# Prompt attention of a hybrid decoder step: operands and heads in one block, probability turn and values one head behind the scores, rope queries and values as fp32r triples

## The reference, cut to what matters

```
q = rms_norm(q_a) @ w_q_b            # 8 heads, 128 nope + 64 rope channels
q_rope = rope(q[..., 128:]) * SCALE ; krope = rope(krope)
q_lat = (q[..., :128] @ w_k_b) * SCALE        # 256 latent channels a head
s = q_lat @ ckv.T + q_rope @ krope.T ; s = where(causal, s, -inf)
p = softmax(s)
mla_out = (p @ ckv) @ w_v_b                   # 128 channels a head
mix = concat(mla_out, pool_out, cross_out) * silu(gate)
x = x + mix @ w_out
```

## Time and profile before

| | |
|---|---|
| median of 3 runs | 1042.87 us (1041.45 to 1044.06) |
| profiled execution, its own time | 1044.82 us |
| its span in the trace | 1043.0 us |
| mean granted PE clock | 0.971 |
| PE, matmul | 957.4 us busy, 92% of the span |
| PEld, weight load (overlaps PE) | 853.2 us, 82% |
| DVE | 543.4 us, 52% |
| ACT | 429.9 us, 41% |
| POOL | 99.1 us, 10% |
| DMA | 155.99 MB, mean 150 GB/s |

### The profile page before, as it was taken

One profiled execution on the slowest core, in us unless ns is written; L12 is line 12 of the kernel. 1 busy time (PEld: TensorE's weight loads), 2 busy tenths in 40 slices (PEclk: granted clock), 3 DMA queues, 4 the chain that ended last, 5 costly groups with the idle time before them and its releaser, 6 DMA issues. The chain is left out here.

```text
span 1043.0 us, 15821 instructions
## 1 busy us (share of the span) xinstructions
PE 957.4 (92%) x5821; PEld 853.2 (82%) x5821; DVE 543.4 (52%) x989; ACT 429.9 (41%) x700; POOL 99.1 (10%) x104
## 2 busy tenths in 40 slices
PE   5989999999899999999999897999558699999996
PEld 5967999999789999999999645888457588888884
DVE  3466244322366688878875264665556542233434
ACT  4774211132314576766664132544355442132310
POOL 0010014022000000000000010211454000000000
PEclk9999999999999999999999898999879799999998
DMA  9864432142714778788763341100243463314222
GB/s 364 287 220 141 154 119 74 62 130 85 294 64 129 245 246 250 241 244 248 240 212 115 147 152 56 31 16 1 101 144 119 182 175 128 121 41 155 68 81 101
DMA packets 75054, 155.99 MB, mean 150 GB/s; under 512 B 9097, under 2 KB 43338, under 8 KB 72985
## 3 DMA queue, kind: packets, MB, share of 16 engines
q1 hardware_dynamic: 74032, 148.16, 43.6%
q10 hardware_dynamic: 944, 6.82, 1.8%
HBM read 143.56 MB, written 11.50 MB: 149 GB/s over the span
## 5 line engine op out<-in xcount | busy, mean ns | idle before, releaser
L165 DVE TENSOR_TENSOR w_lo<-w_raw,w_hi 128x1024 fp32r<-128x1024 f32 (+1 forms) x78 | 96.0, 1230 | 171.7 <-ACT w_hi L158 171.6
L158 ACT ACTIVATE w_hi<-w_raw 128x1024 fp32r<-128x1024 f32 (+1 forms) x78 | 81.9, 1050 | 243.1 <-PE z_acc L68 136.0
L66 PE MATMUL z<-x_hi,w_hi 128*128 128x288 f32 x512 | 154.0, 301 | 0.0
L67 PE MATMUL z<-x_lo,w_hi 128*128 128x288 f32 x512 | 151.2, 295 | 0.0
L68 PE MATMUL z<-x_hi,w_lo 128*128 128x288 f32 x512 | 151.1, 295 | 0.0
L66 PE MATMUL z_acc<-x_hi,w_hi 128*128 128x288 f32 x352 | 104.1, 296 | 0.0
L67 PE MATMUL z_acc<-x_lo,w_hi 128*128 128x288 f32 x352 | 103.8, 295 | 0.0
L68 PE MATMUL z_acc<-x_hi,w_lo 128*128 128x288 f32 x352 | 103.5, 294 | 0.0
L66 PEld LDWEIGHTS z<-x_hi,w_hi 128*128 128x128 f32 x512 | 96.5, 189 | 3.4 <-issue 1.1
L67 PEld LDWEIGHTS z<-x_lo,w_hi 128*128 128x128 f32 x512 | 96.6, 189 | 1.3 <-issue 0.2
L68 PEld LDWEIGHTS z<-x_hi,w_lo 128*128 128x128 f32 x512 | 96.5, 188 | 0.0
(11 more groups left out here) (409 smaller groups left out, 2087.8 us busy)
## 6 DMA issues: line engine op xcount, KB each, us to landing
w_raw<-in_w_feat SPq DMA_DIRECT2D x56, 512.0 KB, 4.3
k_raw<-in_cache SPq DMA_DIRECT2D x128, 192.0 KB, 3.1
v_raw<-in_cache SPq DMA_DIRECT2D x128, 128.0 KB, 2.5
o_raw<-in_w_out SPq DMA_DIRECT2D x32, 512.0 KB, 4.0
w_raw<-in_w_mem_kv SPq DMA_DIRECT2D x16, 512.0 KB, 3.9
gate_spill<-gate_tmp SPq DMA_DIRECT2D x16, 288.0 KB, 3.6
mix<-gate_spill SPq DMA_DIRECT2D x4, 1152.0 KB, 14.6
x_nat<-in_x ACTq DMA_DIRECT2D x4, 1024.0 KB, 8.7
```

What stands on the lines that cost most here:

```text
L66: pe.matmul(out, a[0], b[0], start=start, stop=False)
L67: pe.matmul(out, a[0], b[1], start=False, stop=False)
L158: act.activation(s.whi[:, u % SPL, 0:w], s.wraw[:, u % RAW, 0:w], ACT.Copy).then_inc(s.w_hi, 1)
L165: dve.tensor_tensor(s.wlo[:, u % RAW, 0:w], s.wraw[:, u % RAW, 0:w], f32(s.whi[:, u % SPL, 0:w]), ALU.subtract).then_inc(s.w_lo, 1)
```

## The change

In the middle block: at the step n = 32 (of 38) SP loads `wqr`, `wvb` and the weights of two heads, into room of the key ring; at the last step ACT makes the high part of `wqr` (128x2048), and DVE its low part after all its other work.

In the new block (`attention_stage`):

- rope queries and values of the prompt are fp32r triples, 4 triples and 2 x 2 triples of 512 columns for each row tile; latents, query latents and `wvb` are split for it, `qa_lo` on DVE and no longer on POOL;
- the new tokens' value products come right after the first transposes;
- the rotated rows are written once (two heads make one 128-wide transpose: 4 instead of 8 for each tile), the rope operations have no wait behind each of them; high and low rope queries lie under each other, in 3 ACT and 2 DVE operations of 64 partitions for each tile;
- scores have three PSUM banks instead of two and all four tiles stand in a row; queries and keys of a head have one buffer and no longer two;
- the turn is a plain transpose in three units of 4, 3 and 3 blocks; the division is four ACT copies with a per-row scale (`divide`) after one reciprocal for all four tiles, and no POOL work is left; the negation is folded into the masked maximum;
- the gate product of head h - 2 stands in the middle of head h; SP loads the weights of head h when `project(h - 1)` is done.

```diff
@@ middle_stage, SP, ACT, DVE
+                    if n == QUADS:
+                        sp.wait_ge(sc_ps, QUADS)
+                        sp.dma_start(s.wqr[:], a["w_qr"]).then_inc(wqr_in, 16)
+                        sp.dma_start(s.wvb[:], a["w_vb"]).then_inc(s.wvb_in, 16)
+                        for h in range(2):
+                            sp.dma_start(s.wqk[:, h, :], a["w_qk"][h]).then_inc(s.wqk_in[h], 16)
...
+                    if n == STEPS - 1:
+                        act.wait_ge(wqr_in, 16)
+                        act.activation(s.wqr_hi[:], s.wqr[:], ACT.Copy).then_inc(wqr_done, 1)
...
+                dve.wait_ge(wqr_done, 1)
+                dve.tensor_tensor(s.wqr_lo[:], s.wqr[:], f32(s.wqr_hi[:]), ALU.subtract).then_inc(wqr_done, 1)
+                dve.wait_ge(wqr_done, 2)
                 dve.wait_ge(ot_sb, 2 * DB)
@@ attention_stage, ACT
+                def divide(h, i):
+                    act.wait_ge(inv, h + 1)
+                    act.activation(p_rows(h, i), p_rows(h, i), ACT.Copy, scale=st[:, h % 2, 2, i:i + 1]).then_inc(scaled, 1)
...
                 for h in range(NH + 1):
                     if h < NH:
+                        exps(h, 0)
+                        exps(h, 1)
                     if h:
                         turned(h - 1, 0)
                         turned(h - 1, 1)
                     if h < NH:
+                        exps(h, 2)
+                        exps(h, 3)
+                    if h + 2 < NH:
+                        weights(h + 2)
+                    if h + 1 < NH:
+                        queries_keys(h + 1, 0)
                     if h:
                         turned(h - 1, 2)
+                    if h < NH:
+                        divide(h, 0)
+                        divide(h, 1)
+                    if h + 1 < NH:
+                        queries_keys(h + 1, 1)
+                    if h < NH:
+                        divide(h, 2)
+                        divide(h, 3)
@@ attention_stage, DVE
+                def inverses(h):
+                    dve.wait_ge(exped, 4 * h + 4)
+                    dve.reciprocal(st[:, h % 2, 2, :], st[:, h % 2, 1, :]).then_inc(inv, 1)
...
+                rope(0)
+                values_low(0)
+                rope(1)
+                rope_low(0)
+                values_low(1)
                 weights(0)
+                rope(2)
+                rope_low(1)
+                values_low(2)
+                rope(3)
+                rope_low(2)
+                values_low(3)
+                queries_keys(0, 0)
+                queries_keys(0, 1)
+                rope_low(3)
                 weights(1)
...
                 for h in range(NH + 1):
                     if h < NH:
                         maxima(h, 0)
                         maxima(h, 1)
...
                     if h:
                         turned(h - 1, 0)
                         turned(h - 1, 1)
                     if h < NH:
                         maxima(h, 2)
+                        maxima(h, 3)
+                    if h >= 2:
+                        gate(h - 2)
+                    if h + 2 < NH:
+                        weights(h + 2)
+                    if h < NH:
+                        inverses(h)
+                    if h + 1 < NH:
+                        queries_keys(h + 1, 0)
                     if h:
                         turned(h - 1, 2)
+                    if h + 1 < NH:
+                        queries_keys(h + 1, 1)
@@ attention_stage, PE
+                    for k in range(4):
+                        last = product(pe, q_bank(i), [t[:, k, P * i:P * i + P] for t in (qah, qal)],
+                                       (s.wqr_hi[:, k, :], s.wqr_lo[:, k, :]), k == 0, k == 3)
...
+                rope_queries(0)
+                rope_queries(1)
+                values_of(0)
+                turn_rope(0)
+                rope_queries(2)
+                values_of(1)
+                turn_rope(1)
+                rope_queries(3)
+                values_of(2)
+                turn_rope(2)
+                values_of(3)
+                project(0, 0)
+                project(0, 1)
+                turn_rope(3)
+                pe.wait_ge(tq_lo, 8)
...
                 for h in range(NH + 1):
                     if h < NH:
+                        for i in range(4):
+                            scores(h, i)
                     if h:
+                        turn(h - 1, 0)
+                        turn(h - 1, 1)
+                    if h + 1 < NH:
+                        project(h + 1, 0)
                     if h:
+                        turn(h - 1, 2)
+                    if h + 1 < NH:
+                        project(h + 1, 1)
+                    if h:
                         values(h - 1)
```

More of the change, by code:

```diff
@@ L1251, in _ @@
                     sp.dma_start(s.mix[:, 4 * c:4 * c + 4, :], s.spill[4 * c:4 * c + 4].rearrange("k p t -> p k t")).then_inc(s.mix_in, 16)
[L1253 to L1260, removed]
+                for h in range(2, NH):
+                    sp.wait_ge(qk_ps, 2 * (h - 1))
+                    sp.dma_start(wr[:, h % 2, :], a["w_qk"][h]).then_inc(w_in[h % 2], 16)
             @block.gpsimd
@@ L1446, in _ @@
+                act.activation(kst[ROPE:P, :], p_s[0:ROPE, 2, :], ACT.Copy).then_inc(kr_hi, 1)
+                latents(2)
+                latents(3)
+                act.wait_ge(ct_ps, 1)
+                for c in range(2):
+                    act.activation(cth[:, c, :], p_qk[:, c, :], ACT.Copy).then_inc(ct_hi, 1)
+                act.wait_ge(s.wvb_in, 16)
+                for c in range(2):
+                    act.activation(wvh[:, c, :], s.wvb[:, c, :], ACT.Copy).then_inc(wv_hi, 1)
                 weights(0)
@@ new lines, in values_of @@
+                def values_of(i):
+                    for j in range(2):
+                        if i:
+                            pe.wait_ge(v_lo, 2 * i - 1 + j)
+                        else:
+                            pe.wait_ge(ct_lo, 2)
+                            pe.wait_ge(wv_lo, 2)
+                        for c in range(2):
+                            last = product(pe, p_qk[:, j, :], [t[:, c, P * i:P * i + P] for t in (cth, ctl)],
+                                           [t[:, c, 512 * j:512 * j + 512] for t in (wvh, s.wvb_lo)], c == 0, c == 1)
+                        last.then_inc(v_ps, 1)
@@ L1560, in scores @@
[L1560 to L1572 removed]
+                    if h:
+                        pe.wait_ge(nmax, 4 * (h - 1) + max(i, 1) + 1)
@@ new lines, in scores, with turn @@
+                    out = sc_rows(i, n)
+                    pe.matmul(out, qst[:, h, rows], kst[:, 0:n], start=True, stop=False)
+                    pe.matmul(out, qst[0:ROPE, h, rows], klo[:, 0:n], start=False, stop=False)
+                    product(pe, out, (qkh[:, 0, rows], qkl[:, 0, rows]), (qkh[:, 1, 0:n], qkl[:, 1, 0:n]), False, True).then_inc(sc_ps, 1)
+                def turn(h, u):
+                    unit = 3 * h + u
+                    pe.wait_ge(scaled, 4 * h + 4)
+                    if unit >= 2:
+                        pe.wait_ge(t_lo, unit - 1)
+                    out = t_unit(h, u)
+                    blocks = ([(i, 0) for i in range(4)], [(i, 1) for i in range(1, 4)], [(3, 3), (2, 2), (3, 2)])[u]
+                    for n, (i, j) in enumerate(blocks):
+                        last = pe.transpose(out[:, P * n:P * n + P], pr[:, h % 2, TRI[i] + P * j:TRI[i] + P * j + P], s.ident[:])
+                    last.then_inc(t_ps, 1)
@@ L1584, in values @@
                     last.then_inc(o_ps, 1)
-                project(0)
+                for i in range(4):
+                    last = pe.transpose(p_s[0:ROPE, 2, P * i:P * i + P], s.kvn[:, i, KVR:KV], s.ident[:])
+                last.then_inc(kr_ps, 1)
+                for i in range(4):
+                    for c in range(2):
+                        last = pe.transpose(p_qk[:, c, P * i:P * i + P], s.kvn[:, i, P * c:P * c + P], s.ident[:])
+                last.then_inc(ct_ps, 1)
+                pe.wait_ge(s.wvb_in, 16)
@@ new lines, in _ @@
+                for h in range(NH):
+                    for c in range(2):
+                        last = pe.matmul(p_o[:, NS * h:NS * h + NS], s.wvb[:, c, DV * h:DV * h + DV],
+                                         s.olt[:, c, h, :, :].rearrange("p b t -> p (b t)"), start=c == 0, stop=c == 1)
+                last.then_inc(vb_ps, 1)
+                rope_queries(0)
[3 more added lines that the diff above has]
+                rope_queries(2)
```

473 lines of the change are left out of this document (201 added, 272 removed).

## The result

The change makes the kernel slower: 1049.05 us, the median of 20 runs (1043.68 to 1054.54), against 1043.72 us (1040.23 to 1045.74, 20 runs) for the kernel before. The ratio is 1.0059, 95% interval 1.0044 to 1.0075. The forecast was 1030.2 us, faster. The profiled execution of the changed kernel took 1048.8 us; its span is 1047.0 us.

The account below looks back on a forecast made before the run. PE, busy 92% of the span, was taken as the bound, with ACT and DVE setting the new loop's period. Terms 2.2 - 16.8 - 3.1 + 5.0 = -12.7 took 1042.87 to 1030.2 us; range 1021 to 1038.5.

Parts of the forecast that it names:

- third term: Attention loop, 97.9 us before: ACT and DVE set the period, heads go from 12.44 to 11.8 us; -3.1 us.
- fourth term: Clock: idle at the barrier and before the first scores brings two 1.2 GHz stretches of 2.5 us; +5.0, bounds 0 and 10.
- barrier: First term, end of middle block: DVE's `wqr_lo` behind `qm` delays PE's start by 2.2 us.
- opening: Second term, PE's first transpose to first scores, 55.6 us before: work -7.1, waits -4.7, slow clock -5.0, together -16.8.
- waits in it: Opening: PE waits 2.3 us for low values before `project(0, 0)` and 3.2 us before the first scores, replacing 10.2 us.
- first head: Loop: the first head gets longer, 9.0 for 7.5 us, because its keys are late.
- The division: ACT in the loop: 0.73 us taken for 512 columns; 0.62 would give 11.55 us a head and 1.9 us less.
- The loads ahead of the last values: Before the barrier: three loads, some 7 us, only eat slack; 0 taken, +3 the bound.
- A: Rival, loop: PE sets the period, heads of 10.5 us, no slow stretch; 1016 us, chance 0.12.
- B: Rival, loop: gains nothing, small divisions or a later reciprocal cost 0.6 us a head, one more slow stretch; 1037, chance 0.19.
- C: Rival, loop: clock falls in every head, 1.2 GHz for half the loop; 1057 to 1062 us, slower, chance 0.07.
- D: Rival: `probs` transposes take two passes, triples no faster; 0.3 us a head, 1033, counted within the forecast's 0.62.

Follow-up runs that it names:

- k128: The change with zero rows under the low rope keys, so their score matmul has 128 rows instead of 64; 1030.37 us, ratio 0.988 to the kernel before.
- all_four_mm: all_four with each transpose of the turn done as a plain fp32 matmul by the same identity; 1020.22 us, ratio 0.9783 to the kernel before.
- k128_w_late: k128 with DVE's `wqr_lo` ahead of the fill's last piece and the head weights' split out of mid-head; 1022.14 us, ratio 0.978 to the kernel before.
- all_four: k128_w_late with the opening reordered: last rope turn before the first `project`, last low values earlier on DVE; 1015.44 us, ratio 0.9717 to the kernel before.

## Why the prediction was wrong, step by step

**The step that failed** is in the third term: "PE's work in a head: scores 1.19 + 2.13" was carried over from the trace of before although the change replaces one of the five matmuls of each tile. L1559 had 128 rows; L1601 has 64. It was costed by its columns alone, as if fewer rows could at worst gain nothing. It costs 1.55 us in a head, and all of it is on the path, since the scores stand on the chain that the forecast itself laid out ("scores 3.3", then the turn, ACT and DVE): 8 x 1.55 = 12.4 us. k128 shows it: with this one term put right the head falls from 13.15 to 11.59 us, where 11.8 were forecast.

**The fourth term** was too small as well: +5.0 against the 5.0 of before, that is no net change, where the two profiles show some 5 us more in the block and the clock of all runs says 8 to 9 us. Its two stretches in the opening came. Not foreseen were those in the first heads, which cost 3 us in each (the first head took 13.6 us and k128's 9.1, the second, by the starts of its and the next scores, 665.95 - 650.07 = 15.9 and 11.6; each less 1.55 for the rows). What brought them stays open; the table above shows how far the 64 rows go with them. Together: 12.4 + 5.7 = 18.1, near the 17.8 by which the loop exceeded its 94.8. The change ended 18.0 us away from the forecast difference (+5.3 and -12.7); that the two agree so well is luck, since the opening's low clock cost 1 us less than allowed and the medians differ by 1.3 us more than the profiles.

**What held** is best seen in k128, which has just this step put right:

| | forecast | change | k128 |
|---|---|---|---|
| barrier, us more | +2.2 | +2.4 | +2.4 |
| opening | 38.8, slow clock apart | 42.6 | 42.6 |
| waits in it | 2.3 and 3.2 | 2.19 and 3.40 | 2.18 and 3.40 |
| first head | 9.0 | 13.6 | 9.1 |
| a head | 11.8 | 13.15 | 11.59 |
| loop | 94.8 | 112.6 | 95.0 |
| median | 1030.2 | 1049.05 | 1030.37 |

The opening's 42.6 is close to 38.8 and the two stretches of low clock inside it, some 1.7 us each. The division took 0.71 us for 512 columns, near the 0.73 taken. The loads ahead of the last values cost nothing, as forecast. That k128 fell within 0.2 us of 1030.2 is partly luck, since its runs spread over 7.6 us, and its own expectation of 1036 to 1038 missed it.

**The rivals.** A was wrong for this change; its head of 10.5 us came as soon as the head weights left the chain. B and C came nearer in size and had the wrong cause: the head did grow, but by PE's own work and not by ACT or DVE, and the clock fell in two heads and briefly at the loop's end, not in half of the loop. D did not happen: a transpose is one record; had it, all_four_mm puts the price at 1.08 us in a head where PE is the bound, not 0.3. None of the rivals had a mechanism by which a matmul of the same columns gets dearer; that one was missing.

**Open**: what decides between one, two and no stretch of low clock behind the opening, run by run; and what inside PE takes the 0.19 us. The middle block of both kernels has many matmuls of 64 rows as well; giving them 128 was not tried.

## What to carry to other kernels

Before an operand's shape is taken as free, compare both numbers of the shape with those of the neighbours, rows as well as columns, and look for any place in the trace where such a mixture already runs; here it ran 8 us ahead of the block. Zero rows that keep all matmuls at one row count cost nothing that these runs could see, and took 14 to 19 us off; where they can't be had, put the odd ones side by side. A list of PE work whose terms are "unchanged" deserves the same line-by-line check as the terms that change.

## What the runs showed that was not expected

A change between 128 and 64 rows of consecutive matmuls costs about 0.19 us at 2.4 GHz, as the mean of both directions: in three pairs of kernels 1.53 to 1.57 us for 8 changes in a head, and in one 0.79 us for 4. A matmul of 256 columns otherwise takes 0.12 us. At such a change the weight load doesn't start before its own matmul.

Small waits and small PE stalls can be worth more than their length, through the granted clock: mending 4.1 us of waits in the opening took some 11 us off the change and 6.7 us off k128_w_late. The stalls of the 64 rows came with 6 us more than their own 12.5 in the change, with 1.7 in all_four, and with less than 1 in the kernel before, so no fixed surcharge can be read from this.
